# The delta rule's steps in two staggered halves, with the normed tokens' low parts made on GpSimd

## The reference

```python
def step(state, inp):
    q_i, k_i, u_i, w_i, g_i, a_i = inp
    v_new = u_i - w_i @ state
    o_i = (q_i * jnp.exp(g_i)[..., None]) @ state + a_i @ v_new
    g_last = g_i[..., -1]
    k_dec = k_i * jnp.exp(g_last[..., None] - g_i)[..., None]
    state = state * jnp.exp(g_last)[..., None, None] + jnp.einsum('bhcd,bhce->bhde', k_dec, v_new)
    return state, o_i
_, o = lax.scan(step, s0, xs)
```

## Time and profile before

| | us |
|---|---|
| timed runs | 1574.41, 1574.36, 1570.94 |
| median | 1574.36 |
| profiled execution, its time | 1570.56 |
| its span in the trace | 1568.9 |
| TensorE busy | 1531.0 (98%) |
| VectorE busy | 907.5 (58%) |
| ScalarE busy | 550.0 (35%) |
| GpSimd busy | 98.1 (6%) |
| TensorE clock granted | full in all 40 slices |

### The profile page before, as it was taken

One profiled execution on the slowest core, in us unless ns is written; L12 is line 12 of the kernel. 1 busy time (PEld: TensorE's weight loads), 2 busy tenths in 40 slices (PEclk: granted clock), 3 DMA queues, 4 the chain that ended last, 5 costly groups with the idle time before them and its releaser, 6 DMA issues.

```text
span 1568.9 us, 30359 instructions
## 1 busy us (share of the span) xinstructions
PE 1531.0 (98%) x12808; PEld 1346.4 (86%) x12808; DVE 907.5 (58%) x1395; ACT 550.0 (35%) x851; POOL 98.1 (6%) x106
## 2 busy tenths in 40 slices
PE   9999999999999999989999999999999989999998
PEld 8999999999998679977888888888888877776777
DVE  6655245665479787555444655533555565557872
ACT  6322122232245573024223332222223144436960
POOL 0000000000001460000000000000000000000410
PEclk9999999999999999999999999999999999999999
DMA  7443333345423200002222222223322253111001
GB/s 283 145 142 112 108 109 134 139 118 133 128 65 105 62 2 31 5 4 80 94 100 100 107 81 107 82 92 108 107 82 90 98 218 127 66 63 55 2 9 74
DMA packets 27668, 147.71 MB, mean 94 GB/s; under 512 B 2928, under 2 KB 3328, under 8 KB 16944
## 3 DMA queue, kind: packets, MB, share of 16 engines
q1 hardware_dynamic: 21616, 122.50, 22.4%
q0 software_dynamic: 5424, 22.68, 5.3%
q10 hardware_dynamic: 528, 1.08, 0.2%
HBM read 140.97 MB, written 5.27 MB: 93 GB/s over the span
## 4 chain that ended last, share of the span: by engine, by line
PE 85%; DVE 8%; ACT 3%; issue 2%; DMA 1%; POOL 1%; SPq 0%; DVEq 0%; ACTq 0%
PE PS L660 24%; PE PS L661 24%; PE PS L662 24%; PE PS L1151 1%; PE PS L1086 1%; PE PS L1136 1%; PE PS L1046 1%; PE PS L1149 1%; ACT PB L1688 1%; DVE WLO L1910 1%; PE PS L959 1%; PE PS L1060 1%; DMA SILUC<-in_c 1%; DMA H<-in_h 1%; DVE TAB L2122 1%
## 5 line engine op out<-in xcount | busy, mean ns | idle before, releaser
L660 PE MATMUL PS<-UH,WHI 128*128 128x264 f32 (+1 forms) x1088 | 326.8, 300 | 2.9 <-DVE WLO L1910 2.9
L661 PE MATMUL PS<-UH,WLO 128*128 128x264 f32 (+1 forms) x1088 | 325.4, 299 | 0.0
L662 PE MATMUL PS<-UL,WHI 128*128 128x264 f32 (+1 forms) x1088 | 325.0, 299 | 0.0
L1413 ACT ACTIVATE WHI<-RAW 128x2048 fp32r<-128x2048 f32 (+3 forms) x124 | 210.3, 1696 | 296.1 <-PE PS L662 293.9
L1910 DVE TENSOR_TENSOR WLO<-RAW,WHI 128x2048 fp32r<-128x2048 f32 (+3 forms) x124 | 251.2, 2025 | 77.2 <-ACT WHI L1413 76.5
L660 PEld LDWEIGHTS PS<-UH,WHI 128*128 128x128 f32 x1088 | 204.7, 188 | 10.1 <-DVE WLO L1910 2.5
L661 PEld LDWEIGHTS PS<-UH,WLO 128*128 128x128 f32 x1088 | 204.6, 188 | 6.5 <-issue 0.2
L662 PEld LDWEIGHTS PS<-UL,WHI 128*128 128x128 f32 x1088 | 204.3, 188 | 6.2
L660 PE MATMUL PS<-UHS,WHI 128*128 128x512 f32 x520 | 204.3, 393 | 0.8 <-DVE WLO L1910 0.8
L662 PE MATMUL PS<-ULS,WHI 128*128 128x512 f32 x520 | 202.4, 389 | 0.0
L661 PE MATMUL PS<-UHS,WLO 128*128 128x512 f32 x520 | 202.4, 389 | 0.0
(11 more groups left out here) (440 smaller groups left out, 2696.7 us busy)
## 6 DMA issues: line engine op xcount, KB each, us to landing
RAW<-in_f2u SPq DMA_DIRECT2D x22, 1024.0 KB, 4.8
RAW<-in_f1u SPq DMA_DIRECT2D x21, 1024.0 KB, 4.8
ADA<-in_ada POOLq DMA_DIRECT2D x24, 512.0 KB, 4.7
RAW<-in_f1d SPq DMA_DIRECT2D x16, 704.0 KB, 4.1
RAW<-in_f2d SPq DMA_DIRECT2D x16, 704.0 KB, 4.0
RAW<-in_wi SPq DMA_DIRECT2D x10, 1024.0 KB, 4.8
RAW<-in_w SPq DMA_DIRECT2D x8, 1024.0 KB, 4.8
RAW<-in_mg SPq DMA_DIRECT2D x8, 1024.0 KB, 4.8
```

The source lines that it names most:

```text
L660: mm(out, WHI[:, slot, c:c + w], hi, start=first, stop=False)
L661: mm(out, WLO[:, slot, c:c + w], hi, start=False, stop=False)
L662: return mm(out, WHI[:, slot, c:c + w], lo, start=False, stop=last)
L1413: A(WHI[:, slot, 0:w], RAW[:, slot, 0:w], ACT.Copy).then_inc(hi_rdy, 1)
```

## The change

Three edits.

1. The scan's products are issued in two halves of the tiles, (0, 1) and (2, 3), with semaphore counts of their own; the second half uses banks 4 and 5. Output tiles of the step before or of this one stand between the halves.
2. SE is gone. The new state is made by one scalar_tensor_tensor a tile, SV times the decay plus PSUM, 64 columns.
3. `low(2, n)` is gone from VectorE's loop. GpSimd makes each low part as two operations, gain times H into a buffer and that minus the high part: tiles 3 to 7 after the fourth level of group 0, tiles 0 to 2 after the last level of group 1.

```diff
@@ gpsimd
+        for x, k in enumerate((3, 4, 5, 6, 7, 0, 1, 2)):
+            if k == 3:
+                pool.wait_ge(uh_rdy, KD * (ROUND[2] + 1))
+                pool.wait_ge(t_rdy, 4 * SIDE + 1)
+            elif k == 0:
+                pool.wait_ge(a_ps, NB * LEVELS)
+            if x >= 2:
+                pool.wait_ge(ul_rdy, KD * ROUND[2] + x - 1)
+            gained = CT1[:, x % 2, 0:SEQ]
+            G1(gained, H[:, k, N_META:T1], col(GAIN[2], k), None, ALU.mult).then_inc(px_d, 1)
+            pool.wait_ge(px_d, 39 + x)
+            G2(UL2[:, k, :], gained, UH2[:, k, :].bitcast(f32), ALU.subtract).then_inc(ul_rdy, 1)
@@ tensor
+        def delta_keys(n, half):
+            pe.wait_ge(st_rdy, 2 * n + half + 1)
+            for t in (2 * half, 2 * half + 1):
+                for p in range(2):
+                    last = mm(PS[rows_of(p), 4 * half, t * CH:(t + 1) * CH], KBG[rows_of(p), t * NCH + n, :],
+                              SV[rows_of(p), n % 2, t, :], start=True, stop=True)
+            last.then_inc(ws_ps, 1)
+        def delta_state(n, half):
+            pe.wait_ge(vn_rdy, 2 * n + half + 1)
+            if n == NCH - 1:
+                return
...
+        def delta_out(n, t):
+            if n >= 2 and t == 0:
+                pe.wait_ge(o_ev, n - 1)
...
+            if t == 3:
+                last.then_inc(o_ps, 1)
         for n in range(NCH):
-            pe.wait_ge(st_rdy, n + 1)
...
+            for half in range(2):
+                delta_keys(n, half)
+                if n:
+                    delta_out(n - 1, 2 + half)
+            for half in range(2):
+                delta_state(n, half)
+                delta_out(n, half)
+        for t in (2, 3):
+            delta_out(NCH - 1, t)
+        pe.wait_ge(ul_rdy, KD * (ROUND[2] + 1))
@@ vector
-        dve.sem_inc(st_rdy, 1)
+        dve.sem_inc(st_rdy, 2)
         for n in range(NCH):
-            if n < NCH - 1:
-                egl = GPB[:, :].rearrange("p (t n) -> p t n", n=NCH)[:, :, n:n + 1].to_broadcast([P, 4, CH])
-                TT(SE[:, :, :], SV[:, n % 2, :, :], egl, ALU.mult).then_inc(se_rdy, 1)
             if n >= 2:
                 dve.wait_ge(o_ps, n - 1)
-            dve.wait_ge(ws_ps, n + 1)
-            TT(VN[:, n % 2, :, :], chunk_of(VB, n), ws, ALU.subtract).then_inc(vn_rdy, 1)
-            if n < KD:
-                low(2, n)
...
+            for half in range(2):
+                ts = slice(2 * half, 2 * half + 2)
+                dve.wait_ge(ws_ps, 2 * n + half + 1)
+                TT(VN[:, n % 2, ts, :], chunk_of(VB, n)[:, ts, :],
+                   PS[:, 4 * half, 2 * half * CH:2 * (half + 1) * CH].rearrange("p (t c) -> p t c", c=CH),
+                   ALU.subtract).then_inc(vn_rdy, 1)
+            if n == NCH - 1:
+                break
+            if n >= 1:
+                dve.wait_ge(o_ps, n)
+            for half in range(2):
+                dve.wait_ge(st_rdy, 2 * n + half + 1)
+                dve.wait_ge(sa_ps, 2 * n + half + 1)
+                for t in (2 * half, 2 * half + 1):
+                    last = STT(SV[:, (n + 1) % 2, t, :], SV[:, n % 2, t, :], GPB[:, t * NCH + n:t * NCH + n + 1],
+                               PS[:, 1 + 4 * half, t * CH:(t + 1) * CH], ALU.mult, ALU.add)
+                last.then_inc(st_rdy, 1)
```

More of the change, by code:

```diff
@@ L347, in build @@
     out_st, cs_n = sem("out_stored"), sem("cmp_probs_scaled")
-    sink_s, se_rdy = sem("sink_shifted"), sem("state_decayed")
+    sink_s = sem("sink_shifted")
     kd_rdy, rx_rdy = sem("decayed_keys_ready"), sem("factors_repeated")
@@ L1169, in _ @@
         pe.wait_ge(w_rdy, NB)
-        for n in range(NCH):
-            pe.wait_ge(st_rdy, n + 1)
[L1173 to L1182, removed]
-            if n < NCH - 1:
[L1184 to L1198, removed]
@@ new lines, in rows_of @@
+        def rows_of(p):
+            return slice(CH * p, CH * (p + 1))
+        def delta_keys(n, half):
[10 more added lines that the diff above has]
+            for t in (2 * half, 2 * half + 1):
+                for p in range(2):
+                    last = mm(PS[rows_of(p), 1 + 4 * half, t * CH:(t + 1) * CH], KDEC[rows_of(p), t * NCH + n, :],
+                              VN[rows_of(p), n % 2, t, :], start=True, stop=True)
+            last.then_inc(sa_ps, 1)
@@ new lines, in delta_out @@
+        def delta_out(n, t):
+            if n >= 2 and t == 0:
+                pe.wait_ge(o_ev, n - 1)
+            for p in range(2):
+                o = PS[rows_of(p), 2 + n % 2, t * CH:(t + 1) * CH]
+                mm(o, SV[rows_of(p), n % 2, t, :], GB[rows_of(p), t * NCH + n, :], start=True, stop=False)
+                last = mm(o, VN[rows_of(p), n % 2, t, :], IT[rows_of(p), t * NCH + n, :], start=False, stop=True)
+            if t == 3:
+                last.then_inc(o_ps, 1)
+        for n in range(NCH):
+            for half in range(2):
[5 more added lines that the diff above has]
+                delta_out(n, half)
@@ L2514, in _ @@
         chain(V.memset(SV[:, 0, :, :], 0.0))
-        dve.sem_inc(st_rdy, 1)
+        dve.sem_inc(st_rdy, 2)
         for n in range(NCH):
-            ws = PS[:, 0, 0:4 * CH].rearrange("p (t c) -> p t c", c=CH)
-            sa = PS[:, 1, 0:4 * CH].rearrange("p (t c) -> p t c", c=CH)
-            if n < NCH - 1:
-                egl = GPB[:, :].rearrange("p (t n) -> p t n", n=NCH)[:, :, n:n + 1].to_broadcast([P, 4, CH])
-                TT(SE[:, :, :], SV[:, n % 2, :, :], egl, ALU.mult).then_inc(se_rdy, 1)
             if n >= 2:
                 dve.wait_ge(o_ps, n - 1)
-            dve.wait_ge(ws_ps, n + 1)
-            TT(VN[:, n % 2, :, :], chunk_of(VB, n), ws, ALU.subtract).then_inc(vn_rdy, 1)
-            if n < KD:
-                low(2, n)
[L2529 to L2535, removed]
+            for half in range(2):
[11 more added lines that the diff above has]
+                dve.wait_ge(sa_ps, 2 * n + half + 1)
+                for t in (2 * half, 2 * half + 1):
+                    last = STT(SV[:, (n + 1) % 2, t, :], SV[:, n % 2, t, :], GPB[:, t * NCH + n:t * NCH + n + 1],
+                               PS[:, 1 + 4 * half, t * CH:(t + 1) * CH], ALU.mult, ALU.add)
+                last.then_inc(st_rdy, 1)
         dve.wait_ge(o_ev, NCH)
```

## The result

The kernel after takes 1593.06 us (median of 22 runs, 1568.74 to 1596.15), the kernel before 1573.17 (22 runs, 1570.93 to 1575.84). It is slower. The measured ratio is 1.0101, 95% interval 1.0082 to 1.0119. That ratio leaves out 13 of the 22 runs as slow, and so understates the change (the two medians give 1.0126). 21 of the 22 runs lie between 1590.3 and 1596.2 us at a mean clock of 0.978 to 0.984, and one at 1568.74 with 0.996. The profiled execution took 1590.61 us, 20.1 more than that of before.

What follows compares the result with a forecast made beforehand. TensorE, busy for 98% of the span, was taken as the bound. From 1572.5 us, 5.4 came off for loop and tail and 1.7 were lost to held VectorE operations, net 3.7: 1568.8 us, range 1564.3 to 1573.4.

Steps and rivals of the forecast that it cites:

- The step of the loop: Delta rule's loop: one step with staggered halves takes 2.05 us instead of 2.71, TensorE idling 0.11 of it.
- Loop and tail: Delta rule's loop up to the first product of z: 5.4 us come off in all.
- VN's half: VectorE's subtraction in the loop, at 128 columns instead of 256: 0.29 us.
- the update: State update on VectorE in the loop, one scalar_tensor_tensor of 64 columns a tile: 0.28 us each.
- GpSimd's pair: The two GpSimd operations that make one low part: 2.9 us, including waits.
- its first batch: GpSimd's first five low parts, after group 0's fourth level: from about 625.1 to near 639.8 us.
- No wait for low parts before z: Ahead of z: GpSimd's last low parts end near 675.4 us, 17 us before TensorE asks for them.
- The held operations: VectorE's masks and subtractions ahead of L1136, delayed by GpSimd: 1.7 us lost, bounds 0 and 3.6.
- three meetings at 0.55 us: Three of six VectorE operations fall beside a GpSimd tensor_tensor, each losing 0.55 us.
- the term for GpSimd's meeting: Start of the second doubling group: GpSimd's low parts cost 1.7 us through delayed VectorE operations.
- my list of the six: Three masks (L2459) and three L2477, VectorE operations reading two SBUF operands from 636.16 to 640.38 us, which meet GpSimd.
- The middle place of 1572.5 us: Whole kernel before: runs lie in two places 3.6 us apart; the forecast counts from 1572.5, between them.
- The rival "slower": Six masks and subtractions and a memset before the loop each held 0.92 us, 6.4 in all: 1573.5 us, chance 0.07.

Runs made afterwards that it cites:

- experiment 4: Kernel after with one wait changed, so GpSimd's first batch starts after the second group's masks and first inverses; 1568.01 us, ratio 0.9967.
- 9: experiment 1 with the first inverse of batch 1 in group 1 made three times; 1592.69 us, ratio 1.0122.
- experiment 8: Kernel after with one filler product on TensorE ahead of the second batch's 32-column products; 1568.95 us, ratio 0.9976.
- experiment 7: Kernel after with two filler products on TensorE ahead of the second group's first mask products; 1593.75 us, ratio 1.0133.
- experiment 10: experiment 1 with the mask of batch 0 in group 1 made four times; nine of eleven runs 1568.84 to 1571.90 us, ratio 0.9979.
- 6: experiment 1 with the masks of batches 0 and 1 in group 1 made twice; nine of ten runs 1566.94 to 1570.04 us, ratio 0.9971.
- 12: experiment 1 with the mask of batch 1 in group 1 made four times; 1569.37 us, ratio 0.9982.
- experiment 11: experiment 1 with one product of the inverse in the fourth level's first batch of group 1 made seven times; 1577.35 us, ratio 1.0030.
- experiment 1: Kernel after with the low parts moved from GpSimd to VectorE's waits in the doubling, staggered loop kept; 1567.70 us, ratio 0.9968 to the kernel before.
- 3: Kernel before with its undivided loop, but with the low parts made on GpSimd; 1598.12 us, ratio 1.0161.
- experiment 5: experiment 1 with masks of batches 0 and 1 made twice and first inverse of batch 1 three times, in group 1; median 1594.56 us.
- 2: Staggered loop kept, with VectorE making one low part a step inside it instead of GpSimd; 1569.99 us, ratio 0.9978 to the kernel before.

## Why the prediction was wrong

I forecast 1568.8 us with a range of 1564.3 to 1573.4, and a chance of 0.07 for slower. It is 1593.06.

**Right, by its own steps.** The step of the loop: 2.09 us for a forecast 2.05. TensorE idles for 0.15 us in the whole loop, not 0.11 a step. Loop and tail: 5.1 us off for 5.4. VN's half 0.288 us (0.29), the update 0.278 (0.28), the tail from step 8 to z 717.89 - 715.65 = 2.24 (2.29). GpSimd's pair: 1.56 + 1.27 and a gap, 2.9 us (2.9), its first batch from 625.19 to 640.45 (639.8). No wait for low parts before z. The held operations: 1.9 us (1.7, bounds 0 to 3.6). In experiment 4, where nothing is held, the gain of the loop is all there.

**The port, in detail.** The timeline of the first mask alone:

```profile
636.05 1.23 DVE L2487 TENSOR_TENSOR UMB<-EU,TAB 128x384 f32<-128x384 f32 x1
```

It starts at 636.05 and takes 1.23 us, which is its 0.55 from 636.73 on; GpSimd's L630 ended at 636.86. L2505 starts at 639.48 and ends at 640.86, its 0.55 from 640.31 on; L630 ended at 640.45. Both waited out a GpSimd tensor_tensor, nearly to its end. In between the tensor_scalar took 2.31 us instead of 1.56, and of the two masks beside it the second took 0.55 us and the third 0.96, so held by 0.40; the prediction had an operation beside a tensor_scalar as unheld. The Trainium skill, "SBUF — State Buffer", section "SBUF: two separate sides", has the port pair as a lock for the whole instruction; for the two-input operations these rows agree. I had three meetings at 0.55 us, each beside a tensor_tensor. There were two such, of 0.68 and 0.83, and the 0.40 beside the tensor_scalar. That the sum came out near 1.7 is luck in part.

**The step that failed** is the sum of the term for GpSimd's meeting: I priced a late VectorE operation by its lateness alone, "3 x 0.55 = 1.7 us lost", and read the clock of the stretch as given. The range held 3.6 us of lateness and no case in which lateness costs more than itself. It does: at this place 1.9 us of it made a stall of 0.89 us in the 32-column products, and the clock fell for 51.2 us behind it, 23.2 us lost. I also didn't ask where TensorE would stand for the held time. That it would split, and that the second part would fall among other products, was to be expected from what the prediction itself says: TensorE starts L1136 in step with L2479, which follows an L2477 that was on my list of the six.

The middle place of 1572.5 us, from which I counted, was near the median of 1573.17. That was luck too: the place of a run goes with its granted clock, which the prediction didn't look at.

What shows it: the clock falls with the second stall and without GpSimd (9), not with GpSimd and without the second stall (8), nor with GpSimd off the six operations (4); the first stall is neither needed (7) nor mostly enough (10), and the sum of the two doesn't decide (7). The rival "slower" named the right place, the held masks and subtractions, and the wrong price.

**What was in reach.** The profile of before has TensorE at full clock in all slices with one stall of 1.11 us there (the line L1133 above), and says nothing of how near the clock was to falling. The Trainium skill has something near it: "TensorE: Matmul & The Clock Gate", section "A second HAM failure mode: psum-queue depth-cycling", says that short idles between groups of matmuls can be frequent enough for the clock to go up and down, in a kernel that cycles through PSUM banks. In kind this case's traces agree (0.87 to 1.23 us idle, then 0.50). But here one such stall was enough, and the clock didn't come back for 51 us though TensorE had work without a gap. Had I set a case for it, with the 33.5 us from the third batch's L1136 at 640.42 to the loop at half speed, its upper bound would have been 33.5 us (an estimate).

**Open.** Why a single first stall of 1.7 to 2.9 us (6, 10), or a second one among the 64-column products (12), costs the clock in 1 or 2 runs of 10 and the shorter one among the 32-column products in nearly all; whether it is the narrower products around it or its place in time, experiments 11 and 12 don't settle. What ends the low stretch is open too: after 4 to 5 us at 485 in experiment 1, 17 in experiment 11, 51 in the kernel after, and 58 in experiment 10.

## What to carry to other kernels

This is one kernel, and what sets the clock off in it is known only in part. Where TensorE runs small products (here 64x64 and 64x32, with the next operands from VectorE batch by batch), price a new wait of about 1 us twice: as itself, and as the clock at 0.50 for what follows, and read the granted clock by window before any other explanation of a loss. Keep GpSimd's SBUF work out of the stretch in which VectorE's two-input SBUF operations lead TensorE, which here took one changed wait (experiment 4, 1568.01 us), or use VectorE's own waits (experiment 1, 1567.70 us); these two are the fastest versions, 0.3% ahead of the kernel before. If a stall can't be removed, two filler instructions in it held the clock here (experiment 8, 1568.95 us), while four in the stall ahead of it didn't (experiment 7).

## What the runs showed of the hardware

- A stall of 0.87 to 1.23 us among 64x32 products: by time and mean clock TensorE's clock fell in 21 of 22 runs of the kernel after, 4 of 4 in each of experiments 3, 7 and 9, and 8 of 10 in experiment 5. In the five that were profiled it went to 0.50 1.0 to 2.3 us behind the stall and stayed there for 51 to 55 us, while TensorE was busy in all of a window of 50.00 us. In experiment 11, with 1.47 us later on, it stayed for 17 us.
- A stall of 1.71, 2.90, or 1.12 and 1.33 us that lay wholly ahead of or among the 64x64 products: 1 of 10, 2 of 11, 1 of 10 runs (experiments 6, 10, 12). With the stall of 1.1 us alone: none of 25 (experiments 1, 2, 4), and none of 97 of the kernel before.
- The runs of the kernel before spread over 1570.19 to 1577.05 us, and the spread goes with their mean clock of 1.000 to 0.993.
- The same instructions at half the clock: 72 products of 64x32 in 4.08 us for 2.29.
- GpSimd's tensor_scalar with one full-size input takes 1.56 us for 128x512, 3.05 ns a column, more than its two-input tensor_tensor (1.27 us, 2.5 ns).
